# Differential attention with an unscaled first softmax: the second is added with -lambda s0/s1, and the head norm's epsilon takes s0 squared

## The reference, cut to what matters

```python
def diff_mixer(q, k, v, lam, subln, tab, lam_init):
    lam_full = exp(sum(lam[0] * lam[1])) - exp(sum(lam[2] * lam[3])) + lam_init
    def block(qi, qb):
        s = einsum('bthed,bshed->behts', qb, k) * scale + rel_bias(dist, tab)
        p = masked_softmax(s, dist >= 0)          # e = 0, 1: two maps of a head
        a = p[:, 0] - lam_full * p[:, 1]
        o = einsum('bhts,bshd->bthd', a, v)
        o = rmsnorm(o, subln) * (1.0 - lam_init)  # over the 128 features of a head, epsilon 1e-6
```

## Time and profile before

| what | us |
|---|---|
| median of 3 runs | 2308.64 |
| the profiled execution, its own time | 2309.05 |
| its span, first to last instruction | 2307.1 |
| PE busy | 2220.2 (96%) |
| POOL busy | 1368.7 (59%) |
| DVE busy | 1245.1 (54%) |
| ACT busy | 541.6 (23%) |

### The profile page before, as it was taken

How to read it: one execution, slowest core, us unless ns; L and a number is a source line. 1 busy time by engine, 2 the same in 40 slices (tenths; PEclk the granted TensorE clock), 3 DMA queues, 4 the chain that set the end, 5 groups by cost and what they waited for, 6 DMA issues and landing times.

```text
span 2307.1 us, 32871 instructions
## 1 busy us (share of the span) xinstructions
PE 2220.2 (96%) x11594; PEld 1872.1 (81%) x11598; DVE 1245.1 (54%) x2369; ACT 541.6 (23%) x1313; POOL 1368.7 (59%) x850
## 2 busy tenths in 40 slices
PE   7999999999999899999999999999999999999997
PEld 5888888778878788888888888888767879888886
DVE  5554324798876565552256454126577666654323
ACT  2101002318741441100030000004346144101000
POOL 5666666681247466666658666666441755766662
PEclk9999999999999999999999999999999999999998
DMA  5433332310024123333323333333221311333331
GB/s 194 172 91 100 93 93 89 124 55 20 29 92 119 55 65 100 100 92 94 97 74 110 97 94 94 94 92 99 69 69 36 112 58 63 108 92 100 92 93 53
DMA packets 62418, 206.14 MB, mean 89 GB/s; under 512 B 6831, under 2 KB 9263, under 8 KB 61924
## 3 DMA queue, kind: packets, MB, share of 16 engines
q1 hardware_dynamic: 55312, 187.86, 27.1%
q10 hardware_dynamic: 6996, 16.82, 2.2%
HBM read 201.98 MB, written 8.70 MB: 91 GB/s over the span
## 4 chain that ended last, share of the span: by engine, by line
PE 85%; DVE 10%; issue 2%; ACT 2%; POOL 1%; DMA 0%; another core or an unknown queue 0%; SPq 0%; DVEq 0%; POOLq 0%; ACTq 0%
PE bank L784 25%; PE bank L786 25%; PE bank L785 25%; PE bank L1061 3%; PE bank L1044 2%; PE bank L1028 2%; DVE h_lo L1706 1%; DVE ev_logit L1893 1%; DVE top L1990 1%; DVE bank L1767 1%; PE bank L812 1%; DVE x_res L1775 1%; DVE h_lo L1781 0%; DVE h_lo L1929 0%; PE bank L836 0%
## 5 line engine op out<-in xcount | busy, mean ns | idle before, releaser
L635 POOL TENSOR_TENSOR w_lo<-w_raw,w_hi 128x1024 fp32r<-128x1024 f32 (+1 forms) x358 | 866.8, 2421 | 29.9
L784 PE MATMUL bank<-h_hi,w_hi 128*128 128x512 f32 (+1 forms) x2136 | 802.1, 376 | 29.5 <-DVE h_lo L1706 12.2
L633 POOL TENSOR_SCALAR w_hi<-w_raw 128x1024 fp32r<-128x1024 f32 (+1 forms) x358 | 381.3, 1065 | 708.1 <-PE bank L786 537.9
L785 PE MATMUL bank<-h_lo,w_hi 128*128 128x512 f32 (+1 forms) x2136 | 793.6, 372 | 0.0
L786 PE MATMUL bank<-h_hi,w_lo 128*128 128x512 f32 (+1 forms) x2136 | 793.3, 371 | 0.0
L784 PEld LDWEIGHTS bank<-h_hi,w_hi 128*128 128x128 f32 x2136 | 404.7, 189 | 109.5 <-DVE h_lo L1706 12.6
L786 PEld LDWEIGHTS bank<-h_hi,w_lo 128*128 128x128 f32 x2136 | 404.7, 189 | 69.5
L785 PEld LDWEIGHTS bank<-h_lo,w_hi 128*128 128x128 f32 x2136 | 405.0, 190 | 66.9
L784 PE MATMUL bank<-act_hi,w_hi 128*128 128x512 f32 (+1 forms) x792 | 290.1, 366 | 0.0
L785 PE MATMUL bank<-act_lo,w_hi 128*128 128x512 f32 (+1 forms) x792 | 289.4, 365 | 0.0
L786 PE MATMUL bank<-act_hi,w_lo 128*128 128x512 f32 (+1 forms) x792 | 289.4, 365 | 0.0
(11 more groups left out here) (277 smaller groups left out, 2415.0 us busy)
## 6 DMA issues: line engine op xcount, KB each, us to landing
w_raw<-in_w_up SPq DMA_DIRECT2D x176, 512.0 KB, 3.6
w_raw<-in_w_down SPq DMA_DIRECT2D x64, 448.0 KB, 3.3
w_raw<-in_w_down SPq DMA_DIRECT2D x32, 512.0 KB, 3.5
w_raw<-in_w_ev_in SPq DMA_DIRECT2D x19, 512.0 KB, 3.6
w_raw<-in_w_xkv SPq DMA_DIRECT2D x16, 512.0 KB, 3.6
w_raw<-in_w_od_in SPq DMA_DIRECT2D x16, 512.0 KB, 3.6
bias_line_rows<-bias_lines ACTq DMA_DIRECT2D x1, 6400.0 KB
ev_strip<-bias_line_rows ACTq DMA_DIRECT2D x16, 256.0 KB, 3.0
```

Source lines behind the costliest of these rows:

```text
L633: pool.tensor_scalar(w_hi[j][:, 0:cols], raw[j][:, 0:cols], 1.0, 0.0, ALU.mult, ALU.add).then_inc(hi_split, 1)
L635: pool.tensor_tensor(w_lo[j][:, 0:cols], raw[j][:, 0:cols], w_hi[j][:, 0:cols].bitcast(F32), ALU.subtract).then_inc(split_done, 1)
L784: pe.matmul(out, w_hi[j][:, w], hi, start=first, stop=False)
L785: pe.matmul(out, w_hi[j][:, w], lo, start=False, stop=False)
```

## The change

The `diff0` job is neither inverted nor scaled: its exponentials stay as they are, and the exponential's row sum s0 goes to a buffer of its own, `diff_sum` (128 bytes per partition more of the permanent buffers, so that all later ones move up by as much). For the `diff1` job the small instruction at line 1911 multiplies by -lambda and by s0, and the full-size one adds as before. The semaphores `coef_done` and `scaled` go up by two at the `diff1` job. Before the norm of the four heads one 128x16 instruction computes 1e-6 s0 squared, and the first of the ten small instructions takes it from that buffer in place of a constant.

```diff
+    diff_sum = keep.put("diff_sum", [P, 2, D_HEADS * NT], F32)
...
-                     out=(h, slice(0, P), q), turns=e > 0)
+                     out=(h, slice(0, P), q), turns=e > 0, sums=diff_sum[:, 0, NT * h + i:NT * h + i + 1])
...
+                        total = row_sum[:, j % 8, g:g + 1] if info["turns"] else info["sums"]
                         ins = act.activation(prob[:, at:at + w], logits[s % N_LOGIT][:, at:at + w], ACT.Exp, scale=-1.0,
-                                             bias=neg_max[:, j % 8, g:g + 1], accum_out=row_sum[:, j % 8, g:g + 1])
+                                             bias=neg_max[:, j % 8, g:g + 1], accum_out=total)
...
-                if k == 0:
+                if k == 0 and eps is not None:
+                    ins = dve.scalar_tensor_tensor(value, stat, 1.0 / d, eps, ALU.mult, ALU.add)
+                elif k == 0:
...
                 def invert(s):
                     j, k = j0 + s, len(infos[s]["parts"])
+                    if not infos[s]["turns"]:
+                        return
                     dve.wait_ge(exp_done, j + 1)
-                    dve.reciprocal(coef[:, j % 8, 0:k], row_sum[:, j % 8, 0:k]).then_inc(coef_done, 1)
+                    dve.reciprocal(coef[:, j % 8, 0:k],
+                                   row_sum[:, j % 8, 0:k]).then_inc(coef_done, 1 if infos[s]["sums"] is None else 2)
                 def scale(s):
+                    if not info["turns"]:
+                        return
                     dve.wait_ge(coef_done, j + 1)
-                    if phase == 2 and info["turns"]:
-                        w = info["w"]
-                        small(dve.tensor_tensor(coef[:, j % 8, 0:1], coef[:, j % 8, 0:1], lam[:, 0:1], ALU.mult))
-                        dve.wait_ge(scaled, j)
-                        dve.scalar_tensor_tensor(prob[:, 0:w], prob[:, 0:w], coef[:, j % 8, 0:1],
-                                                 probs_of(phase, s - 1)[:, 0:w], ALU.mult, ALU.add).then_inc(scaled, 1)
+                    if phase == 2:
+                        w, r = info["w"], coef[:, j % 8, 0:1]
+                        small(dve.scalar_tensor_tensor(r, r, lam[:, 0:1], info["sums"], ALU.mult, ALU.mult))
+                        dve.scalar_tensor_tensor(prob[:, 0:w], prob[:, 0:w], r,
+                                                 probs_of(phase, s - 1)[:, 0:w], ALU.mult, ALU.add).then_inc(scaled, 2)
                         return
...
-                rsqrt(("sub", 0), NT * D_HEADS, DV)
+                first, eps = diff_sum[:, 0, :], diff_sum[:, 1, :]
+                small(dve.scalar_tensor_tensor(eps, first, EPS, first, ALU.mult, ALU.mult))
+                rsqrt(("sub", 0), NT * D_HEADS, DV, eps)
```

More of the change, by code:

```diff
@@ L440, in kind_of @@
         s = dict(blocks=i + 1, rows=P, w=w, mask=None, k_lo=None, scale=-DH ** -0.5)
-        s.update(opens=True, closes=True, turns=True)
+        s.update(sums=None, opens=True, closes=True, turns=True)
         if kind == "cmp":
@@ L1661, in _, with rsqrt_op @@
             rs_at = [0]
-            def rsqrt_op(k, d, at=0, w=NT):
+            def rsqrt_op(k, d, at=0, w=NT, eps=None):
                 y0, y1, t_sb, y = (rs[:, j, at:at + w] for j in range(4))
@@ L1694, in rsqrt_op, with rsqrt @@
                 rs_at[0] = n_small[0]
-            def rsqrt(key, w, d):
+            def rsqrt(key, w, d, eps=None):
                 dve.wait_ge(stat_done, SQ[key]["stat"] + 1)
                 for k in range(10):
-                    rsqrt_op(k, d, 0, w)
+                    rsqrt_op(k, d, 0, w, eps)
             def pre_norm(s, c):
```

## The result

The changed kernel takes 2317.26 us (median of 5 runs, 2316.64 to 2320.89) against 2308.64: 8.6 us slower, ratio 1.004 with a 95% interval of 1.0026 to 1.0055. The forecast was 2307.5, with a range up to 2309.8. The profiled execution took 2318.3 us, with a span of 2316.3.

What follows compares the result with a forecast made beforehand. TensorE, busy for 96% of the span, was taken as the bound, so only its phase 2 waits for VectorE counted. Wait by wait they summed to -1.1 us, 2308.64 - 1.1 = 2307.5, range 2304.2 to 2309.8.

Steps and rivals of the forecast that it cites:

- The prediction's own test: Sign of being wrong: among others, that the difference lies outside of 1608 to 1770 us.
- Ceiling and removed work: Phase 2: TensorE's four waits for the pair sum, 3.6 us, cap the gain; 13.7 us of VectorE work goes.
- Step 1: Head 1's last pair, wait of 1.05 us at 1651.97: GpSimd wins the port race again, the wait stays, 0 gained.
- Step 2: First pair of the last head, wait at 1678.05: the blocked scaling goes, TensorE starts 0.8 us earlier.
- Step 3: Wait of 0.87 us at 1688.04: 0.53 of it goes, gain up to here 1.33 us.
- Step 4: Phase 2's end, wait of 1.25 us at 1690.28: ScalarE is late next, TensorE goes on 1.14 us earlier.
- Epsilon: Added 128x16 instruction at 1702.88, between the phases: about 0.17 us, perhaps a 0.4 us wait, costed at 0.
- slower: Outcome slower by 4.6 us: needs three more low-clock stretches or a stall in another stage; chance 0.04.
- The race did not go the other way: Rival at head 1's last pair: small product gets in before w_hi, the 1.05 us wait goes too, 2306.4; chance 0.22.
- The clock's rival: Between the phases and MLA's attention: one more TensorE stretch at 1.2 GHz costs 1.7 us, 2309.2; chance 0.15.
- the edit does nothing on the path: Rival: earlier small products and sums meet GpSimd's splits elsewhere and the gain is eaten up, 2308.6; chance 0.13.
- the four cases: Forecast 2307.5 (0.50), race the other way 2306.4 (0.22), clock 2309.2 (0.15), nothing 2308.6 (0.13).

Runs made afterwards that it cites:

- experiment 1: Kernel before with one unused buffer of 128 bytes per partition behind coef, nothing else of the change: 2318.89 us against 2308.41.
- experiment 2: Changed kernel with 128 unused bytes more behind diff_sum, so later buffers stand 256 bytes above their old place: 2306.55 us against 2308.41.
- experiment 3: Changed kernel with the FFN buffers alone (act_hi, act_lo, gate, up) 128 bytes higher: 2308.45 us against 2308.41.
- experiment 10: Same kernel as experiment 2 (changed, 128 unused bytes behind diff_sum), run again beside experiment 9: 2308.51 us against 2308.85.
- Experiment 9: Changed kernel with the 128 unused bytes and the small product as tensor_scalar with one SBUF input: 2304.72 us against 2308.85.
- experiment 12: Kernel before with the four w_lo tiles 128 bytes higher and everything behind them 256: 2336.68 us (one run).
- experiment 6: Kernel before with act_lo (and gate, up behind it) 128 bytes higher, act_hi unmoved: 2310.25 us against 2308.99.
- experiment 7: Kernel before with act_hi and act_lo 32, 64, 128 and 192 bytes higher in the four FFNs: 2319.32 us (one run).
- experiment 8: Kernel before with act_hi and act_lo 256, 384, 96 and 160 bytes higher in the four FFNs: 2318.88 us (one run).
- experiment 4: Kernel before with every buffer 128 bytes higher, the weights' tiles too: 2308.48 us against 2308.41.

## Why the prediction was wrong

**The step that failed** is the sentence "The shift of all buffers by 128 bytes moves no transfer and no instruction: 0." It is true of the transfers and instructions, and the conclusion is false: it cost 11.7 us by the traces (4 stages of 2.92, worked out above) and 10.5 us by the times of experiment 1. I had seen the shift and asked only what it starts or delays, not whether an instruction's length depends on its operands' places. No row of before could have told, since all operands there stood alike; a kernel with nothing but the 128 bytes in it would have. The prediction's own test came true: the difference lies outside of 1608 to 1770 us.

**The balance.** Of the profiled executions' spans (2316.3 and 2307.1, so +9.2): +0.1 before the first down projection; +8.8 in three of these and +0.4 around them up to phase 2 (+9.2 there); -0.9 in phase 2 up to its last transposes; +1.1 in the products behind them and +0.6 up to MLA's attention, with stretches at 1.2 GHz in other places; -3.4 in MLA's attention; +2.7 in the rest, where the fourth down projection is +2.9. The terms are rounded. The -3.4 is not the edit's. Before, the stage has 6.8 us at 1.2 GHz from 1720.0 on and lasts 53.8 us; after, it lasts 50.4; in experiment 1, with the instructions of before, 50.5. 6.8 us at 1.2 GHz in place of 2.4 lose 3.4 us of work, just this difference.

**The steps in phase 2**, by the start of the transposes that had waited, each against the 9.24 us by which the phase starts later:

- *Ceiling and removed work.* 3.6 us of waits before, 3.3 after, where 3.1 were forecast. VectorE's work over the 111 us fell by 7.4 us (68.2 less 60.8) and not by 13.7, since the waits for GpSimd pass from the scalings to the small products.
- *Step 1, right, but inferred from one execution.* The race came with the margin that was forecast, the small product at 1657.11 and w_hi 0.03 us later, and GpSimd won; the sum took 2.76 us and TensorE waited 1.01. All four profiled executions with the edit and this form of the product came out so (starts 33 to 36 ns apart). The race from which it was inferred went to VectorE in three of nine executions, so that inference was weaker than the prediction held it.
- *Step 2.* Forecast 0.8, measured 0.82 (1686.47 against 1678.05).
- *Step 3.* Forecast 1.33 in all, measured 1.20.
- *Step 4.* Forecast 1.14, measured 0.94. The mis-sized term is the small product: 0.22 us, and 0.10 more to the next instruction, where I took 0.16 to 0.2 and 0.04. That is 0.13 us on the path at the end of each pair.
- *Epsilon.* Forecast 0.17 and perhaps a wait of up to 0.4, at no cost; 0.33 us, and TensorE is what is waited for afterwards.
- *Two slips in the forecast's own arithmetic.* Two stretches of clock below 2307.5 are 2304.1, and with the 0.6 of spread 2303.5, not 2304.2. Three more stretches (5.1 us) less the 1.1 gained make 4.0 us and not the 4.6 that "slower" needed. Neither touches the miss.

**The rivals.** The race did not go the other way in the changed kernel, nor in experiments 2, 3 and 10. Experiment 9, where the small product no longer takes part in it, shows about what that would have been worth: 1.05 us more in phase 2 (84.00 against 85.05). The clock's rival named a mechanism that exists, as the 1.1 us lost from 1699.1 on show; but its stretches stand elsewhere in every execution (in phase 2 and up to MLA: 1703.0 before, 1688.4 and 1702.1 in experiment 2, 1701.8 in experiment 10), so it is a spread of 1 to 3 us on any single execution rather than a consequence of this edit. That the edit does nothing on the path is refuted by the starts where the sum's race is lost both times, but not against an execution that won it, and not by the run times of experiments 2 and 10. None of the four cases came near the 8.6 us.

## What to carry to other kernels

A new small buffer in front of large ones is an edit to every instruction that reads what is behind it. Put it last, or run the kernel with the unused bytes alone before you judge the change: here 128 unused bytes cost 10.5 us, and 31 VectorE instructions fewer brought at most 1.0 in their stage. Where TensorE sets the time and start-to-start distances are all alike, look at where moving and stationary tiles stand to each other modulo 256 bytes, and keep the distance a multiple of it.

Where VectorE shares its port with GpSimd on the path, write a product of one column with scalar operands, so that it has one SBUF input: that, with the place restored, is the fastest version here (2304.72 us). This is shown for one column alone; a TENSOR_SCALAR of 512 columns did wait beside `w_lo` (2.43 us). And a race of some 40 ns for the port is no fixed fact of a kernel: look at several profiles before a step of a forecast rests on who wins it.

## What the runs showed of the hardware that was not expected

- Full-width fp32r products (128x128 weights, 512 columns, weights loaded for each) start every 226.7 ns when moving and stationary operand lie a multiple of 256 bytes apart, 228.9 at 64 bytes off, 233.3 or 233.4 at 32, 96, 128 and 192, 234.3 at 160 (the moving operand moved). With all products 128 off (the weights moved, 232.4 ns) the kernel takes 2345.63 us in place of 2308.99. The modelled lengths of the products with `act_hi` and `act_lo` are 389 ns before and 395 after.
- With `w_lo` alone 128 off (experiment 12) two kinds of product of three were slow, also the one that has `w_lo` only loaded beside it: this would fit a loading of weights that meets the reading of the moving operand, which was not tried by itself and isn't shown.
- A 128x1 TENSOR_SCALAR on VectorE with two scalar operands took 272 to 274 ns at all 16 places, beside GpSimd's splits too; the SCALAR_TENSOR_TENSOR that it replaces took 0.22 us where it didn't wait and up to 1.98 there (experiment 10).
- In races for the port in which VectorE's start is 33 to 47 ns ahead of GpSimd's, GpSimd won with the later start in 10 of 13 profiled executions (1649.08 against 1649.12, 1657.11 against w_hi behind it in the changed kernel, 1648.84 against 1648.88 in experiment 10, and others) and lost in three, all with 47 ns (experiments 6, 7 and 8); with the same 47 ns it won in experiment 4. A sum that had already been waiting (experiment 9, issued at 1647.74) got in between w_hi and w_lo.
